# The first layer's input projections of three tiles made in one pass

## The reference, cut to what matters

```python
for l in range(DEPTH):                       # DEPTH = 2
    h = rmsnorm(x, norm1_g[l])
    z = h @ w_in[l]                          # the input projections, 1024 x 2824
    zq, zk, zv, zf, gu, gv, c_in, c_b, c_c = jnp.split(z, split_at, axis=-1)
    ...                                      # forgetting attention | gMLP gating | gated causal conv
    x = x + mixed @ w_out[l]
    h2 = rmsnorm(x, norm2_g[l])
    x = x + peer_ffn(h2, w_query[l], sub_keys[l], expert_u[l], expert_v[l])
return rmsnorm(x, final_g)
```

## Time and profile before

| | us |
|---|---|
| median of 3 runs | 2999.53 (2996.11 to 3002.63) |
| the profiled execution, its time | 3007.17 |
| its span from the first to the last instruction | 3005.4 |
| TensorE busy with matmuls | 2384.6 |
| VectorE busy | 1981.6 |
| first indirect DMA of a slot | 119.1 |
| indirect DMA of slots 60, 106 and 236 | 317.8, 463.8, 865.1 |
| last indirect DMA of a slot | 2971.4 |
| bytes moved | 1203.87 MB, mean 401 GB/s |
| granted TensorE clock, mean | 0.829 |

### The profile page before, as it was taken

One profiled execution on the slowest core, in us unless ns is written; L12 is line 12 of the kernel. 1 busy time (PEld: TensorE's weight loads), 2 busy tenths in 40 slices (PEclk: granted clock), 3 DMA queues, 4 the chain that ended last, 5 costly groups with the idle time before them and its releaser, 6 DMA issues.

```text
span 3005.4 us, 38541 instructions
## 1 busy us (share of the span) xinstructions
PE 2384.6 (79%) x12832; PEld 984.9 (33%) x12832; DVE 1981.6 (66%) x4722; ACT 1264.9 (42%) x3737; POOL 1245.7 (41%) x1064
## 2 busy tenths in 40 slices
PE   8768778999886887987886897988797566666665
PEld 6734354534441333332441234233252111111110
DVE  1475746688558766787547866788646777777644
ACT  2145433395334424853333433773434333333333
POOL 0133433344444433444333543544434544554552
PEclk8889888999997998788896899899797766666666
DMA  7799999999999999999999999999999999999997
GB/s 239 262 353 402 415 398 400 399 413 410 409 397 422 415 414 417 421 410 416 417 413 418 413 411 415 406 421 398 419 414 421 420 422 421 421 405 421 421 421 293
DMA packets 226608, 1203.87 MB, mean 401 GB/s; under 512 B 26601, under 2 KB 42473, under 8 KB 95337
## 3 DMA queue, kind: packets, MB, share of 16 engines
q0 software_dynamic: 147456, 1073.81, 86.6%
q1 hardware_dynamic: 78952, 127.60, 11.9%
HBM read 1199.24 MB, written 2.10 MB: 400 GB/s over the span
## 4 chain that ended last, share of the span: by engine, by line
DMA 49%; PE 28%; DVE 8%; ACT 7%; issue 5%; POOL 2%; POOLq 0%; DVEq 0%; ACTq 0%
DMA arena<-in_uv,eidx 42%; PE acc L1343 11%; PE bank L1115 9%; PE bank L1180 7%; DVE arena L1101 4%; DMA unit<-in_w_in 4%; POOL arena L603 2%; DMA unit<-in_w_query 2%; ACT L781 2%; ACT wts L784 1%; ACT L699 1%; ACT diag L790 1%; ACT gelu L781 1%; PE heads L1115 1%; ACT region L699 1%
## 5 line engine op out<-in xcount | busy, mean ns | idle before, releaser
L603 POOL DMA_INDIRECT arena<-in_uv,eidx x1024 | 1209.8, 1181 | 1564.1 <-PE acc L1343 1375.8
L1101 DVE CUSTOM_DVE_ANT_0 arena<-arena,h_nat 128x1024 f32<-128x1024 f32 x1024 | 1255.4, 1227 | 789.8 <-DMA arena<-in_uv,eidx 784.6
L1343 PE MATMUL acc<-arena,diag 64*64 64x512 f32 x8192 | 1377.6, 760 | 473.4 <-ACT diag L790 445.1
L781 ACT ACTIVATE gelu<-dots 128x1 f32<-128x1 f32 x1024 | 206.6, 202 | 1456.6 <-DVE dots L1101 1455.1
L1343 PEld LDWEIGHTS acc<-arena,diag 64*64 64x64 f32 x8192 | 256.6, 154 | 1255.2 <-ACT diag L790 1070.8
L1180 PE MATMUL bank<-hT,unit 128*128 128x256 f32 (+1 forms) x1920 | 396.5, 356 | 23.9 <-DMA unit<-in_w_query 18.4
L790 ACT ACTIVATE diag<-identc,wts 128x64 f32<-128x64 f32 x1024 | 356.1, 348 | 33.6
L1180 PEld LDWEIGHTS bank<-hT,unit 128*128 128x128 f32 x1920 | 305.7, 198 | 191.7 <-issue 146.1
L784 ACT ACTIVATE wts<-gelu,gate 128x1 f32<-128x1 f32 x1024 | 301.4, 294 | 33.2
L1115 PE MATMUL bank<-unit,hT 128*128 128x256 f32 (+1 forms) x640 | 224.7, 487 | 4.7 <-DMA unit<-in_w_out 4.4
L1115 PEld LDWEIGHTS bank<-unit,hT 128*128 128x128 f32 x640 | 115.3, 193 | 128.4 <-issue 115.2
(11 more groups left out here) (129 smaller groups left out, 1413.5 us busy)
## 6 DMA issues: line engine op xcount, KB each, us to landing
unit<-in_w_in SPq DMA_DIRECT2D x55, 1024.0 KB, 18.8
unit<-in_w_query SPq DMA_DIRECT2D x40, 1024.0 KB, 17.2
unit<-in_w_out SPq DMA_DIRECT2D x20, 1024.0 KB, 16.0
arena<-in_uv,eidx POOLq DMA_INDIRECT x1024, 17.2
x<-in_x SPq DMA_DIRECT2D x4, 512.0 KB, 8.8
out<-hT SPq DMA_DIRECT2D x4, 512.0 KB, 5.1
gain<-in_norm_g SPq DMA_DIRECT2D x2, 512.0 KB, 13.6
wsp<-in_w_spatial SPq DMA_DIRECT2D x2, 256.0 KB, 11.1
```

The lines of the kernel that those rows point to most:

```text
L603: nc.gpsimd.indirect_dma_start(arena[:, n % NBUF, :], None, uv, bass.IndirectOffsetOnAxis(ap=eidx[:, seq % 2, j:j + 1], axis=0)).then_inc( ...
L781: nc.scalar.activation(gelu[:, group], dots[:, group], ACT.Gelu_apprx_tanh).then_inc(s_ge, GROUP)
L1101: V.tensor_tensor_reduce(out=uu, in0=uu, in1=h_nat[:, seq % 3, :], scale=1.0, scalar=0.0, op0=ALU.mult, op1=ALU.add, accum_out=dots[:, n % ...
L1343: ins = nc.tensor.matmul(acc[rows][cols * HALF:(cols + 1) * HALF, :], diag[own, n % NBUF, :], arena[own, n % NBUF, D + f * 512:D + (f + 1) ...
```

## The change

The second pass makes the input projections of tiles 1, 2 and 3, where before it made those of tile 1. The third pass (tiles 2 and 3) makes none: it takes over what the second left in SBUF, loads no unit of `w_in` and no `wf`, and begins with the norm of the gMLP gates. What a pass makes is told by a new list `inputs`, here [[0], [1, 2, 3], [], [0, 1], [2, 3]]. The core of the diff:

```diff
+    inputs = [list(tiles) for _, tiles in passes]
+    for p in range(1, NP - 1):
+        if len(inputs[p]) == 1 and passes[p - 1][0] == passes[p][0] == passes[p + 1][0]:
+            inputs[p], inputs[p + 1] = inputs[p] + inputs[p + 1], []
...
-    units = [("G", 0, 0), ("G", 0, 1), ("CC", 0, None), ("CI", 0, None), ("CB", 0, None)]
...
+    units_of = [(in_units if inputs[p] else []) + other_units for p in range(NP)]
...
-        return 5 if nt > 1 else 3
+        return 2 * nt + 1
...
     def pace(p):
         if p <= 2 and len(passes[1][1]) == 1:
             split = (first_slot(2) - 20) * sums_of[1][-1] // (sums_of[1][-1] + sums_of[2][-1])
+            split = min(split, first_slot(1) - 22)
...
+        def runs_of(p):
+
+            ni = len(inputs[p])
+            if wide(p):
+                return [(h_in[p][0], 0, P), (hT[:, :, 0:(ni - 1) * P], P, (ni - 1) * P)]
+            return [(hT[:, :, 0:ni * P], 0, ni * P)]
```

More of the change, by code:

```diff
@@ L178, in step_weights @@
         w += [LEAST] * NORM_STEPS + [4 * P] * (2 * nt) + [LEAST] * GAP
-        for _ in range(NQ):
-            w += unit
+        w += unit(nt) * NQ
         w += [LEAST] * tail_steps(nt)
@@ L429, in wait_unit @@
             return wring[n % UNITBUF][:].rearrange("p (c n) -> p c n", c=DC // 2)
-        squares_before = [4 * first_seq[p] for p in range(NP + 1)]
+        squares_before = [in_seq[p] + 3 * first_seq[p] for p in range(NP + 1)]
+        roots_before = [3 * p + sum(len(tiles) > 0 for tiles in inputs[:p]) for p in range(NP + 1)]
         def idle(n):
@@ L913, in dense @@
-                F = Frow[:, t0 * P:t0 * P + N]
-                last = unit_steps(nt) - 1
-                for name, f in IN:
-                    for e in range(unit_steps(nt)):
+                if ni:
+                    yield from idle(GAP + ni - 1)
+                    z0, z1 = zf[p][0:H, 0, :], zf[p][0:H, 1, :]
+                    b = wait_full(dve, p, "ZF")
+                    is_free(V.tensor_scalar(z0, b[0:H, 0:M], bf[:, l:l + 1], None, ALU.add), p, "ZF")
+                    wait_freed(dve, p, "ZF")
+                    V.scalar_tensor_tensor(out=z1, in0=z0, scalar=-1.0, in1=z0, op0=ALU.mult, op1=ALU.min).then_inc(s_zf, 1)
+                    yield 1
@@ new lines, in dense @@
+                M, hs = ni * P, runs_of(p)
+                if not ni:
+                    yield from idle(GATE_STEPS + GAP)
+                else:
+                    yield from idle(NORM_STEPS)
+                    for i, t in enumerate(inputs[p]):
+                        pe.wait_ge(s_drs, in_seq[p] + i + 1)
+                        for f in range(2):
+                            b = wait_free(pe, p, "T1", i, f)
+                            for c in range(4):
+                                ins = mm(b[:, c * P:(c + 1) * P], x[:, t, (f * 4 + c) * P:(f * 4 + c + 1) * P], drs[:, i, :],
+                                         True, True)
+                            is_full(ins, p, "T1", i, f)
+                            yield 1
+                    yield from idle(GAP)
+                    for i in range(ni):
+                        for f in range(2):
+                            wait_freed(pe, p, "T1", i, f)
+                    pe.wait_ge(s_wf, 16 * in_count(p))
+                    b = wait_free(pe, p, "ZF")
+                    for c in range(DC):
+                        for k, (h, at, width) in enumerate(hs):
+                            ins = nc.tensor.matmul(b[0:H, at:at + width], wf[:, c, :], h[:, c, :], start=c == 0 and k == 0,
+                                                   stop=c == DC - 1 and k == len(hs) - 1, skip_group_check=True)
+                        if c == DC - 1:
+                            is_full(ins, p, "ZF")
+                        if part(c + 1, DC, ni):
+                            yield 1
```

487 lines of the change are left out of this document (295 added, 192 removed).

## The result

The changed kernel takes **3008.55 us** (median of 22 runs, 2998.88 to 3023.26) against 3002.15 us for the kernel before (22 runs on the same chips, 2996.11 to 3009.27). The ratio is **1.0018 [1.0009, 1.0026]**: some 5 us slower, with an interval that leaves out 1 and stays under 0.3%, where I had forecast 18 us faster. The time lies above my range, 2965 to 3005. One execution of the last kernel under "Whole kernels" took 3151.84 us at a granted clock of 0.683 instead of 0.82 to 0.83, and does not count in the figures given for it.

The account below looks back on a forecast made before the run. The prediction took the kernel to be bound by DMA from 119 to 2971 us. Its terms, -32 + 16 - 5 + 3 = -18 us, applied to the 2999.5 median gave 2981.5 us, range 2965 to 3005.

Parts of the forecast that it names:

- only helps: Third pass: density falls from 863 to 726 a slot, claimed only to help; no number in the sum.
- the credit: Wide input stage: slots landed ahead are used later, absorbing 3 slots, 8 us, of TensorE's 24 us excess.
- Removed: -32: Eleven units of `w_in` no longer loaded: 32 us less DMA time, with 27 as the other end.
- Moved: +16: New input stage: TensorE needs 181 us, DMA 157; the excess less 8 us credit adds 16 us DMA idle.
- One-tile idle: -5: Old one-tile input stage, 179 to 259 us: its DMA idle time goes, 5 us gained, bounds 0 and 5.
- Squeezed attention and queries: +3, bounds 0 and 10: Second pass: attention gets 18 slots instead of 23, queries 8.7 instead of 18; 3 us added for both.
- The slots' times: Predicted issue: slot 60 near 350 us, 106 near 490, 236 near 847; slots 106 to 236 take 365 us.
- The whole saving arrives: Nine buffers absorb TensorE's excess in the input stage and the idle goes: -37 or -30 us; chance 0.10.
- Taken and given back: Input stage: TensorE runs at the upper bound, 195 us, with little credit; near no change, 2994 to 3005; chance 0.17.
- The ring of four banks: Input stage: banks needed again sooner make TensorE wait for VectorE and ScalarE, up to 45 us; 3006 to 3027; chance 0.15.
- No saving at all, the DMA not being the limit in the third pass: Third pass: DMA is not the limit, so no saving; counted under given back.

Follow-up runs that it names:

- last kernel under "Whole kernels": Changed kernel with a 56-slot input stage, tile 1's copies of `P` on VectorE, and an added matmul per head in the third pass's attention: 3001.46 us, 0.9994.
- their control: Kernel before, with tile 1's softmax left out in the second pass in the same way: 3002.97 us, 0.9995.
- the first experiment: Kernel before, with the third pass's eleven `w_in` units each replaced by a DMA of 16 columns, schedule and matmuls kept: 2990.78 us, 0.9955.

## Why the prediction failed, step by step

**Where the sum went wrong.** Term by term, in lost time: the bytes and what goes with them where they stood, -32 forecast, -32.8 found (-27.7 and -5.1); the wide stage, net of the old idle, +11 forecast (+16 - 5), +14.7 found; tile 1's attention and the queries, +3 forecast, +9.1 found; the third pass's attention, nothing forecast, +11.5 found; elsewhere nothing forecast, -3.2 found. The step that failed first is therefore the one that has no number in the sum: that the third pass, made lighter, "only helps". Next comes the squeezed attention of tile 1, and last the credit.

**What bounds the kernel.** I read a DMA share of 1.01 as "the DMA is the limit", though the same row said that TensorE was busy 126 of 131 us, and I wrote that both are at their limit. For the stage that gives up both its loads this did no harm. It matters for where the columns go: TensorE was the second limit, so every later stage had to be asked whether TensorE, at the clock granted there, still had room.

**Removed: -32.** The size was right for bytes and columns together. For the bytes alone, with the columns left, it was 13.5 us.

**Moved: +16.** TensorE's 181 us were right: the stage's products ran from 178.7 to 357.8 us at clock 1.00. The excess over the DMA's need, 24 us, appears as 24.6 us of lost time (4.6 of them the units' higher price, the rest idle). The credit of 8 us was not won back. It needs a stage behind it with room, and in that stage ScalarE was busy 47.6 and TensorE 55.1 of 61 us. I had written "nothing if attention cannot win it back" and then taken the 8.

**One-tile idle: -5.** It went; in 179 to 359 it is part of the 9.9 us that the kernel before lost (80 us at 370 GB/s alone are 9.0 by that measure, some 4.6 of them the units' higher price).

**Squeezed attention and queries: +3, bounds 0 and 10.** Tile 1's attention lost 9.1 us more than before, near the upper bound. My estimate of ScalarE (44 us of work against 46 of DMA) already showed no margin; the runs without the exponential and their control show that it was the limit. The queries lost nothing in the change as made.

**"In the third pass the density falls, which only helps."** It did not: slots 106 to 236 took 375.8 us instead of 365, and 580 to 620 alone lost 12.1, with TensorE at half clock in its first 24 us. I had read the clock only where TensorE was dense, and taken 1.00 for granted elsewhere. The same slot's matmuls stand at 1.09 us in the earlier trace rows and at 1.99 us here. The Trainium skill (TensorE: Matmul & The Clock Gate, What's actually happening) says that activity releases the throttle; here TensorE was busy 20.00 of 20 us at 0.50, so by the busy time of the profile the trace does not agree. That this stretch was lost is shown; that thinner work was the reason is not, as the section above says. So the cause of the largest single miss stays open.

**The slots' times.** Slot 60 came at 327.9, not near 350, though the stage was as long as forecast. A slot is issued when TensorE is done with the one nine before it, and 9 x 3.7 us before the stage's end at 358 is 325: 350 was nearer to the time of its use. And 847 less 490 is 357, not the 365 that the same paragraph gives for slots 106 to 236; the measured 375.8 is over both.

**The rivals.** *The whole saving arrives* is refuted: the nine buffers did not absorb TensorE's excess, the wide stage lost 24.6 us. *Taken and given back* gives the right outcome at 1.0018, though not by its own reason: the stage took 180 us, not 195. *The ring of four banks* is refuted; in the waits from 179 to 359 us TensorE waits for no copy:

```profile
ACT gelu L887 <- DVE dots L1249: 69.8, 36, 7.9
...
ACT ug L774 <- PE bank L1352: 13.2, 4, 5.7
ACT kT L709 <- PE bank L1352: 11.9, 4, 4.2
...
PEld acc L1516 <- ACT diag L896: 4.2, 6, 0.8
```

It is ScalarE that waits for TensorE's banks, as I had argued against that rival. No `w_in` unit stands among these waits, so the wait of the earlier trace rows did go. *No saving at all, the DMA not being the limit in the third pass*: half borne out by the first experiment, since the bytes alone brought 13.5 us there.

**The sum redone** with what was measured: -27.7 for the bytes at the full rate, +14.7 wide stage, +9.1 tile 1's attention, +11.5 third pass's attention, -5.1 in 480 to 580, and -3.2 elsewhere: -0.7. The two profiled executions agree with it: from the first slot's indirect DMA to the last they took 2852.3 us before (119.1 to 2971.4) and 2852.1 after (117.0 to 2969.1), and 2.1 of the 2.3 us between their spans lie in the prologue. The medians say +5 to +6; that rest is not explained. The changed kernel's runs spread over 24 us, those of the kernel before over 13, and the profiled one was among the faster ones. There is a hint: the changed kernel without the bytes of the wide stage, whose profiled execution took 3012.02 us, stood at clock 0.52 over all of 580 to 620 (270 GB/s instead of 291) and took 380.3 us for slots 106 to 236. A longer time at half clock may be what the slower runs have.

## What to carry to other kernels

Where a stretch shows two resources full, say which of the two loads leaves. Here 11.5 MB alone were worth 13.5 us, and with TensorE's columns gone too the whole 32 in that stage.

Moving work from a place where it is a co-limit to one where it is denser makes it the limit; ask of each following stage whether it has room to win back what was lost, since credit is only worth what the next stage can spend. And read the granted clock in every stretch where TensorE is over some 90% busy, dense or not: a stretch that needs TensorE for over half of its time at full clock has no room for half a clock.

## What the runs showed of the hardware

- TensorE's granted clock stood at 0.50 from 580 to 600 us with TensorE busy 20.00 of 20 us; a slot's eight matmuls took 1.99 us against 1.09 at full clock. Twelve 512-column matmuls spread over the steps ahead did not prevent it (0.50 again); with one for each head within the stretch it was 0.89 and 1.00. The same attention with more slots around it stood at 0.77 to 0.91, with TensorE busy 18.5 to 19.8 of 20 us.
- The DMA share hides a partly filled stream: 0.95 at 360 GB/s, 0.90 at 344, 0.86 at 314, while 1.01 stands beside 417 and, where `w_in` units are a fifth of the bytes, beside 397. GB/s is the row to read, with the units' price in mind.
- Bytes can be free: 11 units less in the TensorE-bound stage changed nothing, 1.0023 after 1.0018.
